# The low parts of the down projections' weights: VectorE's subtraction, or an accumulating DMA onto the negated rounded part

## What is computed

```python
def _swiglu(h, w13, w2):
    a, b = jnp.split(h @ w13, 2, axis=-1)
    return (jax.nn.silu(a) * b) @ w2

def _ffn_sublayer(x, mod, s, g, w13, w2):
    return x + 0.5 * mod[:, :, 3 * s + 2] * _swiglu(_modulate(x, mod, s, g), w13, w2)
```

## Time and profile before

| | |
|---|---|
| runs | 3018.28, 3019.69, 3019.98 us; median 3019.69 us |
| profiled execution, first to last instruction | 3016.9 us; its own total is not listed apart, so the runs stand 1.4 to 3.1 us above this span |
| TensorE busy | 2926.4 us, 97% |
| VectorE busy | 2099.7 us, 70% |
| ScalarE busy | 1175.8 us, 39% |
| GpSimd busy | 322.0 us, 11% |
| DMA | 295.64 MB, 31% of the 16 engines' time |
| mean granted TensorE clock | 0.992 of full speed |

### The profile page before, as it was taken

The page is one execution under the profiler, slowest core; times in us unless marked ns, Lnnn a source line. Parts: engine busy times, 40 slices in busy tenths (PEclk is TensorE's granted clock), DMA queues, the critical chain, the costliest instruction groups (busy, mean ns, idle before and its releaser), DMA issues.

```text
span 3016.9 us, 46631 instructions
## 1 busy us (share of the span) xinstructions
PE 2926.4 (97%) x18078; PEld 2695.2 (89%) x18078; DVE 2099.7 (70%) x4086; ACT 1175.8 (39%) x2139; POOL 322.0 (11%) x439
## 2 busy tenths in 40 slices
PE   7999999999999999999999999999999998999998
PEld 3999999988778999998999998688686976999998
DVE  3888987746658988878779774554536546856756
ACT  4333434344556343346344343222222223634433
POOL 1000003110002000012000011210303005100001
PEclk9999999999999999999999999999999999999999
DMA  6344343511002433322323322323122331123221
GB/s 231 122 131 140 102 141 110 174 58 41 29 29 72 148 98 125 125 98 74 116 85 125 98 91 83 112 83 127 56 86 96 92 125 42 54 80 93 72 88 63
DMA packets 87884, 295.64 MB, mean 98 GB/s; under 512 B 10544, under 2 KB 14928, under 8 KB 86768
## 3 DMA queue, kind: packets, MB, share of 16 engines
q1 hardware_dynamic: 66256, 219.36, 22.4%
q0 software_dynamic: 15232, 56.76, 6.1%
q10 hardware_dynamic: 6176, 16.54, 1.5%
HBM read 285.14 MB, written 7.49 MB: 97 GB/s over the span
## 4 chain that ended last, share of the span: by engine, by line
PE 89%; DVE 5%; ACT 3%; issue 2%; POOL 1%; DMA 1%; POOLq 0%; DVEq 0%; ACTq 0%
PE ps L2228 30%; PE ps L2261 20%; PE ps L2394 12%; PE ps L2129 11%; PE ps L2144 3%; PE ps L2665 2%; PE ps L2674 2%; PE ps L2190 2%; PE ps L2451 1%; PE ps L2419 1%; PE ps L2653 1%; PE ps L2201 1%; PE ps L2434 1%; PE ps L2342 1%; DMA ada<-in_ada 1%
## 5 line engine op out<-in xcount | busy, mean ns | idle before, releaser
L2261 PE MATMUL ps<-g,w 128*128 128x320 f32 x4224 | 625.9, 309 | 1.3 <-DVE x L1472 1.3
L2261 PEld LDWEIGHTS ps<-g,w 128*128 128x128 f32 x4224 | 621.5, 188 | 2.3 <-issue 1.5
L2228 PE MATMUL ps<-h,w 128*128 128x320 f32 x3744 | 583.5, 311 | 15.2 <-ACT swu L925 11.8
L2228 PEld LDWEIGHTS ps<-h,w 128*128 128x128 f32 x3744 | 559.3, 189 | 18.6 <-ACT swu L925 12.9
L2228 PE MATMUL ps<-e,w 128*128 128x320 f32 x2808 | 438.6, 310 | 0.0
L2228 PEld LDWEIGHTS ps<-e,w 128*128 128x128 f32 x2808 | 419.9, 188 | 0.0
L1345 DVE TENSOR_TENSOR w<-raw,w 128x1024 fp32r<-128x1024 f32 (+1 forms) x243 | 276.6, 1141 | 187.1 <-ACT w L825 170.0
L2394 PE MATMUL ps<-w,h 128*128 128x512 f32 x1620 | 376.8, 392 | 7.3 <-DVE rk L2015 4.2
L2394 PEld LDWEIGHTS ps<-w,h 128*128 128x128 f32 x1620 | 304.1, 189 | 73.0 <-issue 4.7
L838 ACT ACTIVATE w<-w2s 128x512 fp32r<-128x512 f32 x312 | 193.1, 630 | 267.9 <-DVE w2s L1495 79.9
L825 ACT ACTIVATE w<-raw 128x1024 fp32r<-128x1024 f32 x123 | 128.6, 1062 | 234.0 <-PE ps L2129 124.9
(11 more groups left out here) (256 smaller groups left out, 3629.5 us busy)
## 6 DMA issues: line engine op xcount, KB each, us to landing
raw<-in_ws SPq DMA_DIRECT2D x303, 512.0 KB, 3.6
cond<-in_ada POOLq DMA_DIRECT2D x80, 512.0 KB, 3.8
raw<-in_ws SPq DMA_DIRECT2D x96, 384.0 KB, 3.1
raw<-in_ada SPq DMA_DIRECT2D x32, 512.0 KB, 3.5
cond_em<-in_ada POOLq DMA_DIRECT2D x16, 512.0 KB, 3.8
ada<-in_ada ACTq DMA_DIRECT2D x6, 1024.0 KB, 21.7
rst<-in_state ACTq DMA_DIRECT2D x4, 1024.0 KB, 4.8
out_new_state<-rsx ACTq DMA_DIRECT2D x8, 512.0 KB, 2.6
```

Of the source, the lines that this page charges most:

```text
L2228: mm = pe.matmul(ps[:, 4 * s + bank, 0:HT], w2[:, at // 2, wi, c:c + P], rhs(k, ri), start=start and k + wi + ri == 0, stop=(k == 3 and wi ...
L2261: mm = pe.matmul(pair_half(pr, half), w2[:, slot_of(n), wi, c:c + P], half_of(g2[:, k, ri, :], half), start=k + wi + ri == 0, stop=(k == n ...
```

## The change

Of the 112 down blocks VectorE makes no low part any more. ScalarE rounds the block into `w2[:, slot, 0]` as before and then copies it a second time, rounded and negated, into `w2[:, slot, 1]`; only then does it count `wt_hi`. GpSimd waits for `wt_hi` and issues a DMA that adds the block, read again from device memory, onto that negated part: `raw` minus rounded. TensorE waits for this DMA's semaphore. SyncE no longer waits for VectorE before it refills the `raw` place of a down block. GpSimd's loads of the conditioning matrix are written out step by step, with the new DMAs between them, and FFN 3, which has no such loads, gets a queue of its own.

```diff
+DOWN = [down_block(q, r, 0) + j for q in range(NFFN) for r in range(len(ROUNDS)) for j in range(KD // PER[r])]
+DOWN_AT = {n: i for i, n in enumerate(DOWN)}
+SPLIT_BY_DVE = list(itertools.accumulate(int(n not in DOWN_AT) for n in range(NBLOCKS)))
...
                         sp.wait_ge(wt_hi, m + 1)
-                        sp.wait_ge(wt_lo, m + 1)
+                        if m not in DOWN_AT:
+                            sp.wait_ge(wt_lo, SPLIT_BY_DVE[m])
...
+            def add_down(n):
+
+                i = DOWN_AT[n]
+                slot, cols = slot_of(n), block_cols(n)
+                pool.wait_ge(wt_hi, n + 1)
+                pool.dma_start(w2[:, slot, 1, 0:cols], a["ws"][n][:, 0:cols], accum_op=ALU.add
+                               ).then_inc(low_ld[i % RING], 16)
+
+            def ffn_loads(q):
 
                 pool.wait_ge(h_hi, chunk(NORM_BEFORE[q], 1, KD - 1))
-                for b in range(ADA_AT[q], ADA_AT[q] + ADA_FFN[q]):
+                at, to = (ADA_AT[q], ADA_AT[q] + ADA_FFN[q]) if q < 3 else (0, 0)
+                for b in range(at, min(at + 2, to)):
                     condition_load(b)
+                ahead = [at + 2]
+
+                def conditions(count):
+
+                    for b in range(ahead[0], min(ahead[0] + count, to)):
+                        condition_load(b)
+                    ahead[0] += count
+
+                for r, nf in enumerate(ROUNDS):
+                    d = down_block(q, r, 0)
+                    for u in range(nf):
+                        conditions(ADA_UP[q][F0[r] + u])
+                    for j in range(4):
+                        add_down(d + j)
+                    if r == 0:
+                        conditions(ADA_GATE[q])
+                    for m in range(KD):
+                        if r < LAST and m < 4:
+                            add_down(d + 4 + m)
+                        conditions(int(m < ADA_DN[q][r]))
...
-                act.activation(w2[:, slot_of(n), 0, 0:cols], raw_of("w", n)[:, 0:cols], ACT.Copy).then_inc(wt_hi, 1)
+                ins = act.activation(w2[:, slot_of(n), 0, 0:cols], raw_of("w", n)[:, 0:cols], ACT.Copy)
+                if n in DOWN_AT:
+                    ins = act.activation(w2[:, slot_of(n), 1, 0:cols], raw_of("w", n)[:, 0:cols], ACT.Copy, scale=-1.0)
+                ins.then_inc(wt_hi, 1)
...
-                if last:
-                    split(d + 1)
-                else:
+                if not last:
                     left_third_sum(*nxt)
                     left_low(*nxt, 2)
...
-            def have(n, i=None):
-
-                pe.wait_ge(wt_lo, n + 1 if i is None else i * RING + (n + 1))
+            def have(n):
+
+                if n in DOWN_AT:
+                    pe.wait_ge(low_ld[DOWN_AT[n] % RING], 16 * (DOWN_AT[n] // RING + 1))
+                else:
+                    pe.wait_ge(wt_lo, SPLIT_BY_DVE[n])
```

More of the change, by code:

```diff
@@ L11 @@
+import itertools
 import math
@@ L427, in build @@
         wt_free = sem("wt_free")
+        low_ld = [sem(f"low_ld{i}") for i in range(RING)]
         cc_ld, const_ld = sem("cc_ld"), sem("const_ld")
@@ L696, in condition_load @@
                 pool.dma_start(cond_of(b), a["ada"][2 * KD + b]).then_inc(cond_ld[b % 2], 16)
-            def ffn_conditions(q):
+            def add_down(n):
[5 more added lines that the diff above has]
+            def ffn_loads(q):
                 pool.wait_ge(h_hi, chunk(NORM_BEFORE[q], 1, KD - 1))
-                for b in range(ADA_AT[q], ADA_AT[q] + ADA_FFN[q]):
+                at, to = (ADA_AT[q], ADA_AT[q] + ADA_FFN[q]) if q < 3 else (0, 0)
+                for b in range(at, min(at + 2, to)):
                     condition_load(b)
+                ahead = [at + 2]
[15 more added lines that the diff above has]
+                        conditions(int(m < ADA_DN[q][r]))
             for b in range(2):
@@ L711, in _ @@
                     low_part(0, h, k)
-            ffn_conditions(0)
+            ffn_loads(0)
             pool.wait_ge(wt_free, done(pair_block(0, LAST, ROUNDS[LAST] - 1) + 1))
@@ L757, in _ @@
             norm_pow(2)
-            ffn_conditions(1)
+            ffn_loads(1)
             norm_pow(3)
-            ffn_conditions(2)
+            ffn_loads(2)
             norm_pow(4)
@@ L813, in _ @@
             norm_pow(5)
+            ffn_loads(3)
             norm_pow(6)
@@ L1561, in first_pairs @@
                 seven = not last and f + 1 == CLASSIC[q]
-                if last:
-                    split(d)
-                    split(d + 1)
-                elif seven:
+                if seven:
                     left_low(q, f + 1, n + 2, 0)
@@ L1571, in first_pairs @@
                         left_low(q, f + 1, n + 2, m)
-                else:
+                elif not last:
                     if f:
@@ L1686, in seven_products @@
                     fourth_value()
-                if last:
-                    split(d + 2)
-                else:
+                if not last:
                     left_low(*nxt, 3)
@@ L1706, in seven_products @@
                     first_half_low(f, u)
-                    split(d + 3)
             def ffn(q, l, s):
@@ L1728, in ffn @@
                         if m < 4:
-                            split(d + 4)
+                            pass
                         elif nxt[1] < CLASSIC[q]:
@@ L2283, in ffn @@
                             continue
-                        pe.wait_ge(wt_lo, n + 2)
+                        have(n + 1)
                         if f == 0:
```

## The result

The changed kernel takes 3028.5 us (median of 5 runs, 3026.9 to 3032.5) against 3018.3 us (5 runs, 3017.6 to 3020.0) for the kernel before: a ratio of 1.0035, 95% interval 1.0022 to 1.0047. It is 10.2 us slower. The forecast was 3021.0 us, that is +1.3 us and no difference that can be measured; 3028.5 us lies inside the stated range (3015.5 to 3055 us), but above the forecast's own range of 3015.7 to 3023.7 us.

What follows compares the result with a forecast made beforehand. TensorE, busy 97% of the span, bounds the kernel. Net losses of 0.3 and 1.0 us in FFN 0 rounds 0 and 1 sum to +1.3 us on 3019.69: 3021.0 us; own range 3015.7 to 3023.7, stated range 3015.5 to 3055.

Steps and rivals of the forecast that it cites:

- a window of some 8 us: Before a round's first down block: 8.1 us for the transfer with 768 columns, 7.7 us with 1024.
- L1671's waits fall to 0.9 us: TensorE's waits for VectorE's sum before product 6 fall from 3.4 us to about 0.9.
- the 0.2 to 0.62 us before product 3: Last step of a round: ScalarE's copy still ends 0.62 us before product 3, 0.2 us with 1024 columns; nothing lost.
- rival B: The negated copy makes ScalarE late for product 3 everywhere: 13.5 us, giving 3033 us; chance 0.05.
- the negated copy costs its length in round 0 only: Only in round 0 of FFN 0 is ScalarE already late; there product 3 starts 0.84 us later.
- condition loads behind waits for `wt_hi`: In GpSimd's queue, condition loads now stand behind these waits; counted as nothing, any lateness under cover of TensorE.
- rival C: VectorE's relief is worth more than two waits: 15.2 us of waits gone plus clock, giving 2998 us; chance 0.06.
- I take 5.0 us: Assumed landing time of the accumulating transfer, between bounds of 3.1 and 6.2 us, nearer the upper end.
- Round 2 of FFN 0, "nothing": Transfer lands at 380.1, TensorE wants it at 381.11, so no wait; round 0 of FFN 1 repeats this pattern.
- with 6.2 us ... +4.0: Upper bound of the sum, landing in 6.2 us: +1.5, +2.2 and two times +0.15, +4.0 us in all.
- Rival A: Transfer slower than its window, from 7.7 to 8.1 us on, in all 16 rounds; 3070 us at 10 us; chance 0.25.

Runs made afterwards that it cites:

- again: The changed kernel measured once more, beside other runs of the kernel before: 3027.9 against 3018.7 us.
- order: Changed kernel with GpSimd's accumulating DMAs of a round's first two down blocks ahead of its last step's condition loads: 3019.1 against 3019.0 us.
- ffn0_dve: Changed kernel with the 28 down blocks of FFN 0 split by VectorE as before: 3017.9 against 3018.3 us, 0.9999.
- plain_dma: Changed kernel with the same transfers as plain copies, without the adding: 3019.2 against 3019.0 us, 1.0002.
- late: order, with GpSimd issuing a round's first accumulating DMA only after ScalarE's copies of the second block: 3040.9 against 3018.3 us, 1.0080.

## Why the prediction was right or wrong

**Right:** that TensorE hardly waits for a low part of a down block except in FFN 0 (0.2 us in round 0 of FFN 1, which the prediction put at nothing, 0.4 in `again`); that a first block has a window of some 8 us (7.9 us with 768 columns, 7.5 with 1024, in `order`); that ordinary rounds hide the transfer (`order` and `ffn0_dve`); that L1671's waits fall to 0.9 us; that the 0.2 to 0.62 us before product 3 suffice, so that rival B is nothing; that the negated copy costs its length in round 0 only (3.84 us in place of 3.11); that condition loads behind waits for `wt_hi` are covered. The gain of the prediction's rival C does not exist: with the transfers left out it is 1.4 us. ScalarE became 80 us busier, not 98, since a second copy starts 0.73 us behind the first and the two overlap in the records; VectorE is 102 us less busy (110 forecast), and TensorE's busy time rose by 5.7 us, more than the 3 I allowed, by the clock.

**The step that failed is "I take 5.0 us".** The landing is 7.0 us at the median and 6.6 to 8.0 where it counted. I had bounded it from above by two plain loads one after the other, 6.2 us, both from SyncE's queue. That bound left out what the trace could have told: the same kind of load from GpSimd's queue was measured there at 0.53 us of issue, a refill of `raw` and a condition load go out at the same moment, and the block behind it follows at once on the same queue. `plain_dma` shows the size of the error by itself: even without adding the transfer takes 4.6 us beside this company, against 3.1 for the refill alone. My 5.0 us was thus the price of a plain copy, and the adding, 2.4 us more, was in effect counted at 0.4.

**Two terms hang on it.** Round 2 of FFN 0, "nothing", waits 1.8 us or not at all, by run. And "with 6.2 us ... +4.0" had 0.15 us of clock for each stall, since I priced the stalls as small; behind the 3.71 us of round 1 it is 1.7 us, and behind the 1.77 us of round 2 again.

**One term was missing.** I placed the transfers against TensorE's due times one by one, and never asked whom they delay. In the last down phase of FFN 0 it is the row `crow_em`, which GpSimd issues behind them and which ScalarE wants before the next stage's weights: 1.7 us.

The sum from the measured terms, along the row `again` of the table: +1.7 up to round 0's down products, +2.3 to round 1's, 1.9 of clock behind it, 3.3 between 473 and 891 us (1.9 of them in the down phase with `crow_em`, the rest clock), 2.7 of clock and small waits later: 11.9 us at 2973 us, in a profile 11.1 us above the one of before.

Rival A, a transfer slower than its window, was the right alternative, and its threshold of 7.7 to 8.1 us fits the windows of 7.9 and 7.5 us: `late` took 2.9 us from them, and every round but the first stalled. But A was drawn as all or nothing. The real case lay between it and the forecast: too slow for the rounds that had a condition load in the way (1.8 to 3.7 us in FFN 0, 0.2 us in FFN 1), quick enough by 0.7 to 2.1 us for the rest.

## What to carry to other kernels

An accumulating DMA is no plain load with a flag: here it took twice the engines' time, two thirds more of GpSimd's issue time and half again the landing. Put it in its queue ahead of loads that nobody waits for yet; that alone was worth 9 to 10 us. Look also at what stands behind it in that queue: here `crow_em` went 4.0 us later and took 2.0 us longer, and 1.7 us were lost. And before work is moved from an engine to the DMA engines, ask both what the engine's time was worth (here 1.4 us for a hundred us of VectorE) and whose transfers are in flight at the same moment.

## What the runs showed of the hardware

- An accumulating DMA of 384 KB from HBM onto SBUF landed in 5.1 to 11.0 us, median 6.5 (`order`), or 7.0 in the changed kernel; the same transfer as a plain copy in 3.5 to 8.4, median 4.6. Its packets took 2.1 us on each of 16 engines against 1.1, and its issue 0.89 us of GpSimd against 0.54.
- Halving it to 192 KB shortened the landing of a transfer by 0.4 us only, brought the whole block 0.8 us later (7.3 us behind the first issue against 6.5), and cost GpSimd 0.95 us (median) for each half.
- Waits for such a transfer appeared in no row of their own: of the 15 in `late`, six stood as "issue" and nine under a VectorE instruction that had long ended.
